# A two-layer transformer trunk: the border ahead of the last FFN by halves, softmaxes joined by their first sum, and an earlier square sum

## The reference

```python
s = einsum('bqhcd,bkhcd->bhcqk', q, k) * DIFF_DH ** -0.5
p = softmax(s, axis=-1)                       # two softmaxes, c = 0 and 1
a = p[:, :, 0] - lam * p[:, :, 1]
o = einsum('bhqk,bkhe->bqhe', a, v)
o = rms_norm(o, sub_g) * (1.0 - lam_init)     # per head and query
y = o.reshape(..., D_MODEL) @ w_o
xl = xl + mod_l[5] * y
xl = ffn_half_step(xl, mod_l, 2, ...)         # x + 0.5 gate * swiglu(norm(x))
```

## Time and profile before

| | us |
|---|---|
| median of 3 runs | 2511.36 (2510.3 to 2513.39) |
| profiled execution | 2509.56 |
| its span, first to last instruction | 2507.8 |
| TensorE busy in the span | 2452.6 |
| VectorE, ScalarE, POOL busy | 1658.8, 907.8, 434.8 |
| mean granted clock of TensorE | 0.994 |

### The profile page before, as it was taken

One profiled execution on the slowest core, in us unless ns is written; L12 is line 12 of the kernel. 1 busy time (PEld: TensorE's weight loads), 2 busy tenths in 40 slices (PEclk: granted clock), 3 DMA queues, 4 the chain that ended last, 5 costly groups with the idle time before them and its releaser, 6 DMA issues.

```text
span 2507.8 us, 40983 instructions
## 1 busy us (share of the span) xinstructions
PE 2452.6 (98%) x14665; PEld 2188.8 (87%) x14665; DVE 1658.8 (66%) x2631; ACT 907.8 (36%) x1446; POOL 434.8 (17%) x523
## 2 busy tenths in 40 slices
PE   8999999999899999999999999999899988999999
PEld 7888888888888888999899999999899977788887
DVE  4788668874888857756784748576777784643332
ACT  2333123332633323424442424244555553331221
POOL 0112111212211111000200000002676741000000
PEclk9999999999999999999999999999999999999999
DMA  7545435541155542222222222223111012433332
GB/s 231 160 146 165 133 112 149 160 126 41 39 163 155 163 120 83 59 76 60 67 64 68 71 65 70 68 69 82 45 33 50 25 34 65 125 102 94 92 104 88
DMA packets 367438, 239.51 MB, mean 96 GB/s; under 512 B 8081, under 2 KB 366066, under 8 KB 367346
## 3 DMA queue, kind: packets, MB, share of 16 engines
q1 hardware_dynamic: 366896, 238.12, 32.8%
q10 hardware_dynamic: 450, 0.18, 0.0%
HBM read 236.18 MB, written 2.10 MB: 95 GB/s over the span
## 4 chain that ended last, share of the span: by engine, by line
PE 73%; issue 13%; DVE 7%; POOL 3%; ACT 2%; DMA 1%; SPq 0%; POOLq 0%; DVEq 0%; ACTq 0%
PE pu L1419 46%; PE pu L1640 15%; PE pv L1791 5%; PE pv L1734 1%; POOL ada_acc L817 1%; DVE h_lo L2408 1%; PE pu L1809 1%; DVE xn L2401 1%; PE pu L1828 1%; PE pv L1819 1%; PE pu L1427 1%; DVE mx L2540 1%; PE pu L1460 1%; PE pv L1559 0%; DVE w_lo L2041 0%
## 5 line engine op out<-in xcount | busy, mean ns | idle before, releaser
L1419 PE MATMUL pu<-h_hi,w_hi 128*128 128x512 f32 (+1 forms) x1552 | 450.5, 352 | 1.5 <-DVE w_lo L2041 1.0
L1419 PE MATMUL pu<-h_lo,w_hi 128*128 128x512 f32 (+1 forms) x1552 | 448.1, 350 | 0.0
L1419 PE MATMUL pu<-h_hi,w_lo 128*128 128x512 f32 (+1 forms) x1552 | 447.1, 350 | 0.0
L2041 DVE TENSOR_TENSOR w_lo<-w_raw,w_hi 128x1024 fp32r<-128x1024 f32 (+3 forms) x212 | 282.7, 1335 | 176.3 <-ACT w_hi L890 170.1
L890 ACT ACTIVATE w_hi<-w_raw 128x1024 fp32r<-128x1024 f32 (+3 forms) x212 | 225.3, 1063 | 465.5 <-PE pu L1419 416.4
L2068 DVE SCALAR_TENSOR_TENSOR ada_acc<-ada_raw,cs,ada_acc 128x384 f32<-128x384 f32 x602 | 345.4, 616 | 11.7 <-DVE ada_acc L2068 2.6
L1419 PEld LDWEIGHTS pu<-h_hi,w_hi 128*128 128x128 f32 x1552 | 249.7, 188 | 43.6 <-DVE w_lo L2041 2.0
L1419 PEld LDWEIGHTS pu<-h_hi,w_lo 128*128 128x128 f32 x1552 | 250.6, 188 | 41.2
L1419 PEld LDWEIGHTS pu<-h_lo,w_hi 128*128 128x128 f32 x1552 | 250.1, 188 | 39.8
L817 POOL TENSOR_TENSOR ada_acc<-ada_acc,ada_parts 128x768 f32<-128x768 f32 x86 | 147.4, 1714 | 781.6 <-ACT ada_parts L897 726.7
L2292 DVE SCALAR_TENSOR_TENSOR xT<-pu,gate,xT 128x512 f32 (+3 forms) x144 | 85.9, 632 | 297.4 <-PE pu L1419 294.2
(11 more groups left out here) (289 smaller groups left out, 4940.8 us busy)
## 6 DMA issues: line engine op xcount, KB each, us to landing
ada_raw<-in_ada_w SPq DMA_DIRECT2D x86, 768.0 KB, 4.7
w_raw<-in_ffn_w_in SPq DMA_DIRECT2D x118, 512.0 KB, 3.9
w_raw<-in_ffn_w_out SPq DMA_DIRECT2D x40, 704.0 KB, 4.4
w_raw<-in_ffn_w_in SPq DMA_DIRECT2D x108, 256.0 KB, 3.1
w_raw<-in_diff_w_qkv SPq DMA_DIRECT2D x21, 512.0 KB, 5.3
w_raw<-in_ffn_w_out SPq DMA_DIRECT2D x24, 384.0 KB, 3.2
first_raw<-in_ada_w SPq DMA_DIRECT2D x8, 1024.0 KB, 11.5
w_raw<-in_ffn_w_out SPq DMA_DIRECT2D x24, 320.0 KB, 3.3
```

The lines of the kernel that those rows point to most:

```text
L1419: last = pe.matmul(banks(ch, s_), w[:, j, :], r[:, SEG[s_]], start=(j == 0 and i == 0), stop=(j == k - 1 and i == 2))
L2041: dve.tensor_tensor(w_lo[:, ch, 0:k * P], w_raw[:, ch, 0:k * P], w_hi[:, ch, 0:k * P].bitcast(F32), ALU.subtract).then_inc(split_ready[ch], 1)
```

## The change

- Border 5 becomes wide (`WIDE` and `NEXT` take in 5) with the halves of 256 tokens as parts. `W_o`'s fourth pair gets slots of its own in attention's space, and the last FFN's first pair goes through `next_raw` and `first_ahead`. SP issues both once the last head's value product is done (`pv_done`). `first_unit` and `tail_dve` go.
- `combine` no longer divides by the first sum: with z0, z1 the sums, a becomes e0 + e1 * (z0 / z1 * nlam), that is z0 times the former. The norm behind it takes the factor out again, with EPS times z0 squared in EPS's place (`keep_eps`, once a head); the scaling of e1 over 768 columns goes.
- In the second head's stage the first tile's square sums stand ahead of its maxima.

```diff
-        zz = sb("zz", [P, 2, 2])
+        zz = sb("zz", [P, QT, 2])
+        ez = sb("ez", [P, QT])
...
+        wo_skip = sb("wo_skip", [P, HEADS, NL], F32, wo_late)
+        last_raw = sb("last_raw", [P, 2, DC * P], F32, wo_late)
+        last_hi = sb("last_hi", [P, 2, DC * P], F32R, wo_late)
+        last_lo = sb("last_lo", [P, 2, DC * P], F32R, wo_late)
...
-        WIDE = (3, 4)
-        NEXT = (POOL_NORM, 3)
+        WIDE = (3, 4, 5)
+        NEXT = (POOL_NORM, 3, 5)
...
-        def last_slot(t, ch, k):
+        def last_slot(i, t, ch, k):
+            if i == 5:
+                return (last_raw, last_hi, last_lo)[(w_raw, w_hi, w_lo).index(t)][:, ch, :]
             return t[:, ch, KMAX // 2 * P:(KMAX // 2 + k) * P]
...
@@ SP
-                        for f in range(int(n in (0, 1)), 2):
+                        for f in range(int(n in (0, 1, 3)), 2):
                             in_pair(0, f, False)
...
-            for m in range(4):
+            for m in range(OUT_PAIRS - 1):
                 for ch in range(2):
                     load_unit(ch, PAIR_WO + m, wslot(w_raw, ch, DC), wo[:, :, 2 * m + ch, :])
+            sp.wait_ge(pv_done, HEADS)
+            for ch in range(2):
+                sp.dma_start(last_raw[:, ch, :]..., wo[:, :, DC - 2 + ch, :]).then_inc(last_in[ch], 16)
+            load_next(3)
             load_ffn(3)
...
@@ ScalarE
-                                   accum_out=zz[:, i % 2, c:c + 1]).then_inc(exp_done, 1)
+                                   accum_out=zz[:, i, c:c + 1]).then_inc(exp_done, 1)
...
-            for m in range(OUT_PAIRS - 1):
-                for ch in range(2):
-                    split_hi(ch, PAIR_WO + m + 1, DC)
-                square_out(5, PAIR_WO + m, m)
-            tail_act(5)
+            for ch in range(2):
+                split_hi(ch, PAIR_WO + 1, DC)
+            square_out(5, PAIR_WO, 0)
+            wide_hi(5, 1)
+            wide_act(5)
             norm_act(5)
...
@@ TensorE
-                        if k == 1:
+                        if k:
                             first_ahead(FFN_IN[k], b)
-                        elif k:
-                            first_unit(FFN_IN[k], b, True)
...
-            for m in range(1, OUT_PAIRS - 1):
-                for ch in range(2):
-                    unit(ch, PAIR_WO + m, DC, lambda j: h_hi[:, j], lambda j: h_lo[:, j], NL)
-            tail_pe(5)
+            for ch in range(2):
+                unit(ch, PAIR_WO + 1, DC, lambda j: h_hi[:, j], lambda j: h_lo[:, j], NL)
+            wide_pe(5)
...
@@ VectorE
-                step(dve.reciprocal(rz[:], zz[:, i % 2, :]))
-                step(dve.tensor_tensor(rz[:, 1:2], rz[:, 1:2], nlam[:], ALU.mult))
-                step(dve.tensor_scalar(e[:, i % 2, 1, :], e[:, i % 2, 1, :], rz[:, 1:2], None, ALU.mult))
+                step(dve.reciprocal(rz[:, 0:1], zz[:, i, 1:2]))
+                step(dve.scalar_tensor_tensor(rz[:, 1:2], zz[:, i, 0:1], rz[:, 0:1], nlam[:], ALU.mult, ALU.mult))
                 dve.wait_ge(ta_done, 2 * n + 1)
-                dve.scalar_tensor_tensor(a[:], e[:, i % 2, 0, :], rz[:, 0:1], e[:, i % 2, 1, :], ALU.mult,
+                dve.scalar_tensor_tensor(a[:], e[:, i % 2, 1, :], rz[:, 1:2], e[:, i % 2, 0, :], ALU.mult,
                                          ALU.add).then_inc(a_ready, 1)
...
-                dve.tensor_scalar(ovar[:], pu[:, 3, 0:QT], 1.0 / DV, EPS, ALU.mult, ALU.add).then_inc(ovar_ready, 1)
+                dve.scalar_tensor_tensor(ovar[:], pu[:, 3, 0:QT], 1.0 / DV, ez[:], ALU.mult, ALU.add).then_inc(ovar_ready, 1)
+            def keep_eps(step, g, held):
+                if held:
+                    dve.wait_ge(ovar_ready, g)
+                z0 = zz[:, :, 0:1].rearrange("p t o -> p (t o)")
+                step(dve.scalar_tensor_tensor(ez[:], z0, EPS, z0, ALU.mult, ALU.mult))
...
-                    first = do_a and do_b and not do_c and s == 0
-                    if do_a and not first and not ctx_early:
+                    if do_a and not ctx_early:
                         sum_squares(h, s)
...
                     if do_b and s < QT:
                         row_max(step, g, s)
-                    if first:
-                        sum_squares(h, s)
...
                     if do_b and 1 <= s <= QT:
                         weights_lo(g, s - 1)
+                    if do_b and s == QT:
+                        keep_eps(step, g, do_c)
...
-            for m in range(OUT_PAIRS - 1):
+            for m in range(2):
                 for ch in range(2):
                     add_out(ch, PAIR_WO + m, ...)
                     split_lo(ch, PAIR_WO + m + 1, DC)
-            tail_dve(5, lambda ch: split_lo(ch, tail_pair(5) + 1, DC))
+                    if m:
+                        last_lo(5, ch, PAIR_WO + OUT_PAIRS - 1, DC)
+            wide_dve(5, lambda ch: next_lo(ch, tail_pair(5) + 1))
             norm_seg(5, 1, {})
+            for ch in range(2):
+                split_lo(ch, tail_pair(5) + 2, DC)
             ffn_dve(3, None)
```

More of the change, by code:

```diff
@@ L1023, in ffn_act @@
                     if q == 0:
-                        silu_pair(b, 0, n, None if k == 1 else DC, k, p0, [beside(k, p0, lag) for lag in (1, SUM_LAG)], k != 1)
+                        silu_pair(b, 0, n, DC if k == 0 else None, k, p0, [beside(k, p0, lag) for lag in (1, SUM_LAG)], k == 0)
                     for lo, hi, ada in spans(k, p0, int(q == 0), FP - 1, (1, SUM_LAG)):
@@ L1454, in wide_unit @@
                 k, ch = wide_k(i), c % 2
-                hi, lo = (last_slot(w, ch, k).rearrange("p (k c) -> p k c", k=k) if c >= 2 else wslot(w, ch, k) for w in (w_hi, w_lo))
+                xs_hi, xs_lo = (h_hi, h_lo) if i == 5 else (b_hi, b_lo)
+                hi, lo = (last_slot(i, w, ch, k).rearrange("p (k c) -> p k c", k=k) if c >= 2 else wslot(w, ch, k) for w in (w_hi, w_lo))
                 for j in range(k):
@@ L1458, in wide_unit @@
                         amid()
-                    for n, (w, x_) in enumerate(((hi, b_hi), (hi, b_lo), (lo, b_hi))):
-                        last = pe.matmul(wide_bank(c, s_), w[:, j, :], x_[:, j, SEG[s_]], start=(j == 0 and n == 0),
+                    for n, (w, x_) in enumerate(((hi, xs_hi), (hi, xs_lo), (lo, xs_hi))):
+                        last = pe.matmul(wide_bank(i, c, s_), w[:, j, :], x_[:, j, seg(i, s_)], start=(j == 0 and n == 0),
                                          stop=(j == k - 1 and n == 2))
@@ L1484, in one @@
                     for n, (w, x_) in enumerate(((hi, h_hi), (hi, h_lo), (lo, h_hi))):
-                        last = pe.matmul(ps(ch, s_), w[ch][:, j, :], x_[:, j, SEG[s_]], start=(j == 0 and n == 0),
+                        last = pe.matmul(tail_bank(i, ch, s_), w[ch][:, j, :], x_[:, j, seg(i, s_)], start=(j == 0 and n == 0),
                                          stop=(j == DC - 1 and n == 2))
@@ L1514, in first_ahead @@
                 last.then_inc(unit_done[1], 1)
-            def first_unit(i, b, late_ctx):
-                for ch in range(2):
-                    pe.wait_ge(split_ready[ch], b + 2)
-                    pe.wait_ge(psum_used[ch], b + 1)
-                    for j in range(4):
-                        pe.wait_ge(h_ready[0], DC * i + j + 1)
-                        chunk_seg(i, ch, 0, j, DC, h_hi, h_lo)
-                    if late_ctx and ch == 0:
-                        sums_most(i, 1)
-                        sums_last(i, 1)
-                for j in range(4, DC):
-                    pe.wait_ge(h_ready[0], DC * i + j + 1)
-                    for ch in range(2):
-                        chunk_seg(i, ch, 0, j, DC, h_hi, h_lo)
-                    if late_ctx and j == DC - 2:
-                        spread(i, 1)
-                for ch in range(2):
-                    for j in range(DC):
-                        pe.wait_ge(h_ready[1], DC * i + j + 1)
-                        last = chunk_seg(i, ch, 1, j, DC, h_hi, h_lo)
-                    last.then_inc(unit_done[ch], 1)
             def unit(ch, pair, k, rhs_hi, rhs_lo, n, acts=None):
@@ L2250, in block_dve @@
                                 if m:
-                                    last_lo(ch, pair + OUT_PAIRS - 1, kp)
+                                    last_lo(FFN_NORM[k], ch, pair + OUT_PAIRS - 1, kp)
                     else:
@@ L2374, in wide_dve @@
                 norm_seg(i, 0, {1: lambda: wide_chunk(i, 1, 2), 2: lambda: wide_chunk(i, 1, 3), 5: lambda: norm_rms(i, 1)})
-            def tail_dve(i, next_lo):
-                for ch in range(2):
-                    tail_chunk(i, 0, ch)
-                norm_rms(i, 0)
-                tail_chunk(i, 1, 0)
-                norm_seg(i, 0, {0: lambda: next_lo(0), 1: lambda: tail_chunk(i, 1, 1), 2: lambda: next_lo(1),
-                                5: lambda: norm_rms(i, 1)})
             def norm_rms(i, s_):
```

39 lines of the change are left out of this document (21 added, 18 removed).

## The result

The changed kernel took 2495.67 us at the median (2494.97 to 2497.08, 4 runs), the kernel before 2510.89 beside it; the ratio is 0.9938, interval 0.9921 to 0.9955. The forecast was 2496.0. The profiled execution took 2495.53 us with a span of 2493.8, against 2507.8 before.

What follows compares the result with a forecast made beforehand. TensorE, busy for 2452.6 of 2507.8 us, was taken as the bound, with gaps in three stretches. Terms 2.7 + 1.6 + 2.6 + 8.4 = 15.3 us gave 2494.3, about 2496 at the median; range 2492.5 to 2501.

Steps and rivals of the forecast that it cites:

- The stated lower end: Whole kernel: 2492.5 us, with the second head's stage and the last head's at their upper bounds, 2.7 us more gain.
- Second head's stage: Second head's attention stage: 2.7 us gained, POOL's 2.1 from an earlier start plus part of the rest; bounds 0.9 and 4.5.
- if the last context tile binds: Second head's stage, lower bound: POOL's last context tile needs the fifth projection, so only TensorE's own 0.9 us is gained.
- The feared reverse: Second head's stage: the earlier POOL could block VectorE's combination once a tile, giving back up to 4 times 0.4 us.
- Heads three to seven: Their stages: TensorE's five waits for `a`, 0.32 to 0.34 us each, all go: 1.6 us gained; bounds 0 and 1.7.
- Last head's stage: Last head's stage: four VectorE scalings of 0.64 us leave the chain, 2.6 us gained; bounds 1.3 and 3.5.
- The new product per head: Softmax combining: one added four-column VectorE operation per head, some 0.2 us, taken to cost 0; bound 1.6 us.
- The border: W_o's third pair to the last FFN's second pair: second pair starts at 2141.7 instead of 2150.1, 8.4 us gained.
- The rival of the falling clock: New border: TensorE's clock falls there as well, costing about 3 us, so 2499 us; chance 0.27.
- The late copies: Weight copies moved on SP: taken as 0, bounds 0 and 2 us; as rival they bind and slow the kernel, chance 0.05.
- Little at the border: Border: if the sums are late too, it gives 4 us instead of 8.4, so 2500.4 us; chance 0.08.
- POOL keeps the stage: Second head's stage stays bound by POOL, full stages pass their gain on: 12.0 us in all, 2499.4 us; chance 0.10.

Runs made afterwards that it cites:

- `x_p1`: Kernel before with only the second head's stage's square sums moved ahead of the maxima: 2514.64 us, ratio 1.0007.
- `y_p2`: Kernel before with only the cheaper softmax combining, all tiles at their former addresses: 2503.98 us, ratio 0.9969 to before.
- `y_p12`: Kernel before with the cheaper combining and the square sums' move, tiles at their former addresses: 2504.07 us, ratio 0.9973 to before.
- `z_no_squares`: Changed kernel with only the square sums' move undone: 2495.81 us, ratio 0.9935 to the kernel before.
- `z_after`: Changed kernel measured again, unaltered, in the third set: 2497.05 us, ratio 0.9938 to the kernel before.
- `y_pad`: Changed kernel with an unused 32-byte tile, `align`, ahead of `a_hi`, nothing else changed: 2498.73 us, ratio 0.9947 to the kernel before.
- `x_p2`: Kernel before with only the cheaper combining, `align` kept, so staged tiles lay 32 bytes further on: ratio 0.9981 to before.
- `x_p12`: Kernel before with combining and square sums' move, `align` kept, so staged tiles lay 32 bytes further on: ratio 0.9988 to before.
- `x_p3`: Changed kernel with combining and square sums' move taken back, border alone, without `align`, staged tiles moved by 32 bytes: ratio 1.0011 to before.
- `y_p3`: Changed kernel with combining and square sums' move taken back, border alone, `align` added so tiles lie as before: 2503.18 us, ratio 0.9967.

## Why the prediction was right, and where its steps were not

- **The total** was right to 0.3 us, and that closely it was luck. The spans show 14.0 us gained against 15.3, chiefly because the border gave 1.35 less. What made up for it is the last step of the sum: 1.8 us were added for the median, as in the kernel before, and the changed kernel's median lies 0.14 us above its profiled execution. By the medians of the runs side by side the gain is 15.2. The stated lower end, 2492.5, is some 0.9 us below what its own terms give (2496.1 less 2.7).
- **Second head's stage** (2.7; measured 2.6). The size held by luck, the reason did not hold. The step "I take 2.7 us for the stage: POOL's 2.1 plus part of the rest" failed. POOL did start 2.1 us earlier, and alone this gave nothing (`x_p1`, 0.4 us longer), on top of the combining 0.1 (`y_p2` to `y_p12`) to 0.4 (`z_no_squares`). The combining alone gave 2.42 of it (`y_p2`). I had allowed POOL "some 0.3 us in a tile" for the scaling that goes; it was 0.47 in the mean of four tiles, and 0.56 more in the context tiles, for which I had nothing. And my bound "if the last context tile binds" was the true case for the earlier start: POOL's new idle times, 0.64 in the changed kernel and 1.91 in `x_p1`, are waits for VectorE's sums of the last tiles. That part of the stage comes from the projections: in the changed kernel the last sum starts 27.42 us into the stage, before 28.25, 0.8 us earlier where I had 0.9.
- **The port.** The timeline of the changed kernel shows VectorE's combination from 1797.68 to 1798.70 inside a pair of POOL products that takes 1.33 us instead of 0.60. By the rule of the Trainium skill (SBUF — State Buffer, section Who interferes with whom), an exclusive lock on the port pair that the two share, the trace agrees. The feared reverse, VectorE held up by POOL, is small in the changed kernel: 32 combinations have a median of 1.025 us and a longest of 1.184, against 1.019 and 1.020 before. It is larger without the square sums' move, 1.30 us in two tiles, and there it costs the 0.4 us of `z_no_squares`.
- **Heads three to seven** (1.6; measured 2.0). All five waits of 0.32 to 0.34 us are gone from TensorE's timeline. Each was worth 0.41 us: idle time is counted from the end of the matmul before, and without a wait the next one starts before that end. From the last product of the scores to the first turn of `a` it was 0.67 us before (1826.14 to 1826.82) and is 0.27 now (1824.08 to 1824.35). Five times 0.41 are the 2.0; the term should have been taken from starts.
- **Last head's stage** (2.6; measured 3.0, and 2.9 in `y_p2`). Four scalings of 0.64 us fit the size; no run tells the rest, 0.4, from the clock. With the same instructions the stage took 35.2 to 37.0 us in the profiles, and the place of the fall goes with it more than the mean clock:
```profile
2043.33:2080.07 36.74, 28.05 (x156) 21.76 (x156) 23.97 (x48) 15.29 (x32) 2.39 (x2) 0.89 0.01 3
2065.21:2068.62 3.41, 3.41 (x11) 2.72 (x10) 1.15 (x4) 0.79 (x2) 0.92 (x1) 0.50 0.00 0
```
This is `y_p12`, with a fall 21.9 us into the stage. The four kernels with a fall 21 to 23 us into it took 36.5 to 37.0 us; `z_no_squares`, with falls at 6.5 and 16.7 us and a mean clock of 0.88, took 35.6. So this term moves by up to 1.8 us with the clock.
- **The new product per head** (0, bound 1.6). No wait appeared where its stages have none before, so 0 stands.
- **The border** (8.4; measured 7.05 with the clock down, 8.7 with it up). The sum by steps was right to 0.3 us: second pair 41.15 us behind the first matmul, where the steps gave 41.3 to 41.5. (The aside that the border would have given 5.3 without the half-rate stretch before should read 5.1, 8.4 less 3.3, and no run tests it.) The rival of the falling clock came true as to its place, some 2 us behind the wait between the halves, in the changed kernel, in `z_after` and in `y_pad`. Its size was off: 1.7 us measured, twice, against "about 3". I had priced 6.6 us of half rate as 3.3 us of lost work, but for the first 2 us of it TensorE has 0.36 us of products for a step of 0.91 us, and then 0.72: the slower products of the first part went wholly into time that was idle before.
- **The late copies** (0): right; ScalarE waited 1.10 us at 2090.32 and TensorE nowhere. SP issued the last of them at 2088.4 and they took 7.1 us, so all had landed by about 2096, where I had 2103.
- **Little at the border; POOL keeps the stage**: neither came. But POOL does still end the second head's stage: TensorE waits 1.04 us, where the sign that I had named was below 1, and POOL's last two products, stretched by 2.9 us beside VectorE's splittings, are the next thing to look at there.

## What to carry over

A stretched instruction in the trace is a debt of its neighbour: when a VectorE operation goes, compare each POOL row beside it with its shortest twin. The sum of the differences is an upper bound (some 4 us in the four query tiles here, 1.9 came), since the VectorE operation that stays stretches another row. And do not credit an earlier start of an engine before asking what its last input waits for. Price a fallen clock by the work that is late because of it, not by the length of the slow stretch. When one part of a change is undone, the addresses of everything allocated behind it must stay where they were; a stage that no edit touches, timed in every kernel, shows at once when they did not.

## What the runs showed of the hardware that I had not expected

- **The place of a matmul operand in SBUF has a price.** All staged tiles 32 bytes off: matmuls that read `a_hi` and `a_lo` took 395 instead of 389 ns in the last FFN, and the last FFN some 313.7 instead of 310.5 us, in each of four kernels (`x_p2`, `x_p12`, `x_p3`, `y_pad`) and in none of the ten others. It is not only a price: the stretch ahead of attention was 1.4 to 6.5 us shorter with the tiles 32 bytes further on (`x_p2`, `x_p12`, `y_pad`) and 7 to 10 us longer with them 32 bytes nearer the start (`x_p3`, one kernel).
- **Whether the clock falls at a place differs between executions of the same instructions there.** One execution of each kernel was profiled. In the changed border the clock fell in four (the changed kernel, `z_after`, `y_pad` and `x_p3`) and stayed up in two (`y_p3`, `z_no_squares`), each time with a wait of some 1.0 us between the halves of the norm. What decides it stays open.
